# Two blocks on one core: whole Gram products and picked column sums in the delta heads, and an earlier load of gate rows in the first mixer

## Chip, cores and metric

The kernel runs on one core of a Trainium2 chip. The metric is device time in microseconds of one execution. TensorE (PE) multiplies, VectorE (DVE), ScalarE (ACT) and GpSimd (POOL) work element by element, SyncE (SP) issues most of the transfers. Every engine has its own instruction stream; they meet on semaphores.

## The reference

A sequence of 1024 tokens of width 1024 goes through two blocks in fp32, each a mixer and an MLP with residual. The first mixer is a forgetting attention (8 heads of width 64, with a cumulated gate added to the scores) beside a spatial gating unit. The second has a short convolution, a gated delta rule (4 heads of width 128, chunks of 64 tokens) and stick-breaking attention. What matters here, for one delta head and one chunk:

```python
k_beta = k * beta[..., None]
lower = where(strict, einsum('cd,sd->cs', k_beta, k) * decay, 0)
sol = triangular_solve(lower + eye, concat([v * beta, k_beta * exp(g)]))
u, w = sol[..., :Dv], sol[..., Dv:]
attn_intra = where(causal, einsum('cd,sd->cs', q, k) * decay, 0)
```

q and k are scaled to unit length first: l2norm(x) = x * rsqrt(sum(x*x) + eps). The kernel folds these scales and the decay into exponentials of sums of logarithms.

## The kernel before

The kernel is a row of stages. Projections and MLPs split fp32 weights into a high and a low part (GpSimd) and multiply in three products. Between them stand the first mixer (mix1_stage) and the delta stage (delta_stage).

**First mixer.** The attention is done in 32 units, four pairs of heads (hp 0 to 3) by eight query tiles. For a unit TensorE computes scores (L585), VectorE adds the gate rows and takes the row minimum (L723), ScalarE exponentiates, TensorE transposes, and every four units it multiplies with the values. The gate rows of a pair lie in cb[hp % 2], two buffers, and are loaded by SyncE (L564). The four slices of the next projection's weights (early_raw, L569) go to where q of the first pairs lay. SyncE's order is: rows of pair 0, rows of pair 1, a wait for unit 15's scores, the four slices, rows of pair 2, rows of pair 3; the rows of pair 2 have a wait of their own for unit 7, those of pair 3 for unit 15.

**Delta stage.** A head's 1024 tokens lie in 8 tiles of 128, each two chunks of 64. The inverse of each 64x64 triangular matrix is built in levels of doubling block size. X and XT hold the inverse and its transpose, LT the transposed matrix (rows 0 to 63 the even chunk, 64 to 127 the odd one), LQ the corner between the two chunks, and LM0/LM1 LT masked for one level. The inverse is carried on to 128 tokens (XT_whole), with level 6 for the corner. In level j TensorE makes t (X times LM, "t10" is level 1, first half), ScalarE copies it to T1, TensorE makes x and xt (L2246), VectorE subtracts them from X and XT (L2196, L2200; in level 5 into XT_whole, L2204, in level 6 L2208). Each level is done in two halves g = 0, 1 of four tiles.

The work of head h + 1 that prepares its matrices is put by hand into slots (j, g) of head h, in one table per engine (PE_SLOTS, ACT_SLOTS, DVE_SLOTS), with separate lists for head 0 (PE_FIRST and so on) and for a head's end (PE_END). GpSimd runs through POOL_EV. Since each engine works in its order, a waiting instruction holds up all that is behind it. The names used later:

- sqk, sqq: squares of k and q. ssk, ssq: their column sums spread to all rows, by a product with ones (L2235). ssc: the column sums of k squared, one column per tile (L2266). lns: their logarithm.
- g, gb: the gates spread to all rows (L2235, L2275, L2277); gcopy, gbcopy: their copies Gb, GBb. lnk, lnq: logarithms of ssk and ssq in Kb and Qb (L2049).
- rk, rq: -0.5 times the logarithm plus the gates (L2142, L2130). b: four pieces of 8 columns in small. elt0, elt: the exponentials of GBb (L2088).
- ea on VectorE: Qb plus the causal mask (L2152); ea0, ea on ScalarE: its exponentials. er1: exponential of Qb to Gb.
- kk: the Gram products of k (L2306). kq: of k with q (L2314). LT: kk times GBb (L2173). a_t: kq times Qb (L2158). qe: q times Gb.
- kt, vt: transposes of k and v; ktcopy: the copy to kd. vb: v times beta. xi: X from XT by transposing (L2296). w, u: the products with XT_whole (L2255). m1 to m5: the masked LM (L2025), ke, kd: scalings of kd, all on GpSimd.

Banks of PSUM: t in 0 and 1, x in 2 and 3, xt in 4 and 5, the preparation's results in 6 and 7, except kk in 2 and 3; xi is in bank 2. In head 0, ea of both engines stands in level 1 (ACT_LATE, DVE_LATE), and VectorE's next instruction there, a_t, needs it.

## Time and profile before

| | |
|---|---|
| median of 3 runs | 2767.29 us (2765.95 to 2768.79) |
| profiled execution, time | 2766.32 us |
| profiled execution, span from first to last instruction | 2764.6 us |
| mean granted TensorE clock | 0.980 of full |
| delta stage: head 0 to 1, 1 to 2, 2 to 3 (first block product to the next) | 57.32, 50.73, 47.87 us |

Busy time is the sum of an engine's instruction durations. In a timeline a row is a run of equal instructions: start in us from the span's start, time that they cover, engine, line, operation, output and inputs, count, and in brackets the idle time before and what ended it. A product of fp32 operands shows as two records. Times of single rows come from the one profiled execution.

### The profile page before, as it was taken

What the parts mean: (1) busy time and instruction counts of PE and PEld (TensorE: products, weight loads), DVE (VectorE), ACT (ScalarE), POOL (GpSimd) and SP (SyncE); (2) the same over time, 40 slices, a digit from 0 to 9 for tenths busy, and PEclk for the clock granted to TensorE, in tenths of its full rate; (3) what the DMA queues carried; (4) which work ended last, traced back from release to release, by engine and by line L of the source; (5) the groups of instructions that cost most, each with busy time, mean ns of one, the idle gap of its engine ahead of it and who ended that gap; (6) DMA issues with size and microseconds to landing.
All of it is one profiled execution on the core that took longest, in us unless ns stands there. A gap on an engine that the chain in (4) does not pass through costs nothing. (4 is left out here: it accounts for less than half of the span.)

```text
span 2764.6 us, 37035 instructions
## 1 busy us (share of the span) xinstructions
PE 2653.8 (96%) x14091; PEld 2113.2 (76%) x14091; DVE 1232.5 (45%) x1701; ACT 669.8 (24%) x1321; POOL 1143.1 (41%) x909
## 2 busy tenths in 40 slices
PE   7999789999999999999999979898999999999998
PEld 6786447888888888887888767853788888888877
DVE  3133343323333333353743044566125566666658
ACT  3201552200000000024231344465122111111123
POOL 4341135244444444543555322211324555555553
PEclk9999989999999999999999978999999999999999
DMA  3111103111111111121111000000311111111111
GB/s 132 43 50 38 47 1 122 31 46 46 47 51 46 49 49 49 53 89 61 46 46 50 12 2 2 17 1 1 122 31 54 46 49 49 49 49 47 48 57 76
DMA packets 91025, 131.75 MB, mean 48 GB/s; under 512 B 9269, under 2 KB 57632, under 8 KB 90920
## 3 DMA queue, kind: packets, MB, share of 16 engines
q1 hardware_dynamic: 88288, 121.76, 14.7%
q10 hardware_dynamic: 2632, 8.51, 0.8%
q8 instruction: 75, 1.23, 0.2%
q14 instruction: 30, 0.25, 0.0%
HBM read 121.82 MB, written 8.42 MB: 47 GB/s over the span
## 5 line engine op out<-in xcount | busy, mean ns | idle before, releaser
L115 POOL TENSOR_TENSOR w_hi<-w_raw,zero 128x512 fp32r<-128x512 f32 x320 | 380.1, 1188 | 994.5 <-PE bank L1095 450.5
L1093 PE MATMUL bank<-xt_hi,w_hi 128*128 128x512 f32 x1232 | 479.4, 389 | 0.8 <-DVE x_sb L1326 0.8
L1094 PE MATMUL bank<-xt_lo,w_hi 128*128 128x512 f32 x1232 | 479.3, 389 | 0.0
L1095 PE MATMUL bank<-xt_hi,w_lo 128*128 128x512 f32 x1232 | 479.3, 389 | 0.0
L117 POOL TENSOR_TENSOR w_lo<-w_raw,w_hi 128x512 fp32r<-128x512 f32 x320 | 464.9, 1453 | 25.1
L1430 DVE TENSOR_TENSOR x_sb<-bank,x_sb 128x512 f32<-128x512 f32 x320 | 221.2, 691 | 203.5 <-PE bank L1129 203.2
L1093 PEld LDWEIGHTS bank<-xt_hi,w_hi 128*128 128x128 f32 x1232 | 231.2, 188 | 49.2 <-DVE x_sb L1326 1.2
L1095 PEld LDWEIGHTS bank<-xt_hi,w_lo 128*128 128x128 f32 x1232 | 231.2, 188 | 48.0
L1094 PEld LDWEIGHTS bank<-xt_lo,w_hi 128*128 128x128 f32 x1232 | 231.2, 188 | 48.0
L1388 DVE COPY hidden_raw<-bank 128x512 f32<-128x512 f32 x44 | 30.4, 692 | 326.0 <-PE bank L1095 325.9
L178 PE MATMUL bank<-xt_hi,w_hi 128*128 128x512 f32 x448 | 174.6, 390 | 0.0
L178 PE MATMUL bank<-xt_hi,w_lo 128*128 128x512 f32 x448 | 174.3, 389 | 0.0
L178 PE MATMUL bank<-xt_lo,w_hi 128*128 128x512 f32 x448 | 174.3, 389 | 0.0
L1397 DVE SCALAR_TENSOR_TENSOR hidden_conv<-hidden_raw_conv,cols,hidden_conv 128x1024 f32<-128x1024 f32 x80 | 156.0, 1979 | 6.6 <-ACT hidden_conv L1230 1.3
L1127 PE MATMUL bank<-w_hi,hidden_hi 128*128 128x512 f32 x320 | 124.5, 389 | 0.0
L1128 PE MATMUL bank<-w_hi,hidden_lo 128*128 128x512 f32 x320 | 124.5, 389 | 0.0
L1127 PE MATMUL bank<-w_hi,hidden_hi_conv 128*128 128x512 f32 x320 | 124.5, 389 | 0.0
L1128 PE MATMUL bank<-w_hi,hidden_lo_conv 128*128 128x512 f32 x320 | 124.5, 389 | 0.0
L1129 PE MATMUL bank<-w_lo,hidden_hi 128*128 128x512 f32 x320 | 124.5, 389 | 0.0
L1129 PE MATMUL bank<-w_lo,hidden_hi_conv 128*128 128x512 f32 x320 | 124.5, 389 | 0.0
L1222 ACT ACTIVATE hidden_raw<-bank 128x512 f32<-128x512 f32 x44 | 26.3, 599 | 360.9 <-PE bank L1095 360.9
L1388 DVE COPY hidden_raw_conv<-bank 128x512 f32<-128x512 f32 x44 | 30.3, 691 | 165.7 <-PE bank L1095 165.7
(535 smaller groups left out, 4814.7 us busy)
## 6 DMA issues: line engine op xcount, KB each, us to landing
w_raw<-in_w_gate_up_dram SPq DMA_DIRECT2D x88, 256.0 KB, 3.1
w_raw<-in_w_ffn_up_dram SPq DMA_DIRECT2D x88, 256.0 KB, 3.1
w_raw<-in_w_mix_in_dram SPq DMA_DIRECT2D x56, 256.0 KB, 2.7
w_raw<-in_w_down_dram SPq DMA_DIRECT2D x44, 256.0 KB, 2.6
w_raw<-in_w_ffn_down_dram SPq DMA_DIRECT2D x44, 256.0 KB, 2.5
w_raw<-in_w_in_dram SPq DMA_DIRECT2D x40, 256.0 KB, 2.7
x_sb<-in_x_dram SPq DMA_DIRECT2D x4, 1024.0 KB, 8.3
gate_rows<-gate_sums SPq DMA_DIRECT2D x8, 512.0 KB, 6.8
```

The source lines that it names most:

```text
L115: pool.tensor_tensor(m.w_hi[:, u, :], m.w_raw[:, u, :], zeros, ALU.add).then_inc(m.hi_done, 1)
L117: pool.tensor_tensor(m.w_lo[:, u, :], m.w_raw[:, u, :], m.w_hi[:, u, :].bitcast(F32), ALU.subtract).then_inc(m.split, 1)
L178: mm = pe.matmul(m.psum[b][:, :], lhs, rhs, start=k == 0 and i == 0, stop=k == KD - 1 and i == 2)
L1093: pe.matmul(m.psum[b][:, :], u_hi[:, col], m.xt_hi[:, k, tok], start=k == 0, stop=False)
L1094: pe.matmul(m.psum[b][:, :], u_hi[:, col], m.xt_lo[:, k, tok], start=False, stop=False)
L1095: mm = pe.matmul(m.psum[b][:, :], u_lo[:, col], m.xt_hi[:, k, tok], start=False, stop=k == KD - 1)
L1127: pe.matmul(m.psum[bank][:, :], hi[:, j, tok], w_hi[:, u, :], start=j == 0, stop=False)
L1128: pe.matmul(m.psum[bank][:, :], lo[:, j, tok], w_hi[:, u, :], start=False, stop=False)
L1129: mm = pe.matmul(m.psum[bank][:, :], hi[:, j, tok], w_lo[:, u, :], start=False, stop=j == 1)
L1388: dve.tensor_copy(raw[:, 2 + j, PAD + h * HALF:PAD + (h + 1) * HALF], m.psum[2 * q_ + 1][:, :]).then_inc(ev_d, 1)
L1397: ins = dve.scalar_tensor_tensor(mix[:, c, :], raw[:, c, PAD - back:PAD - back + S], weights_of(i, c, 2 - back), mix[:, c, :], ALU.mult, A ...
L1430: dve.tensor_tensor(xs, m.psum[t][:, :], xs, ALU.add).then_inc(dn_ev, 1)
```

## The change

In the delta stage:

- kk becomes 8 products of 128x128 (both chunks of a tile and the corner at once, in banks 2 and 3, by tile) instead of 24 of 64 columns. LT and LQ then read their blocks out of them, each in two halves by bank. LQ is an event of its own, last in the start of a head; the x products of level 1, which write banks 2 and 3 again, wait for it.
- ssc and its logarithm on ScalarE go. Instead VectorE multiplies Kb (the logarithms, the same in all rows) by the identity and adds up each 128 columns, which picks the diagonal (lns).
- level 0's mask for XT moves to GpSimd (m0), ahead of m1; VectorE keeps the subtraction from the identity.
- ea writes to a buffer of its own (Qm) instead of Qb, and moves from slot (6,0) to (5,0). In head 0 it moves from level 1 to before xi.
- xi goes to bank 6, and kq waits for its copy.
- the slots close up: g, gb, ssk, ssq, kt, vt come half a level or more earlier on TensorE.

In the first mixer, SyncE issues the gate rows of pair 2 ahead of the four slices.

```diff
-            if hp == 1:
+            if hp == 2:
                 sp.wait_ge(scored, at_piece[(15, 1, 1)] + 1)
                 for u in range(RING):
                     sp.dma_start(early_raw[:, u, :], w_out(u)).then_inc(m.loaded[u], 16)
...
-    PE_SLOTS = {(2, 0): [("ssc", 1)], (2, 1): [("g", 1)], (3, 0): [("gb", 1)], (3, 1): [("ssk", 1)],
-                (4, 0): [("ssq", 1)], (4, 1): [("kt", 1)], (5, 0): [("vt", 1)], (6, 0): [("kk", 1)]}
-    ACT_SLOTS = {(1, 0): [("sqk", 1)], (1, 1): [("sqq", 1)], (2, 0): [("lns", 1)], (2, 1): [("gcopy", 1)],
-                 (3, 0): [("gbcopy", 1)], (3, 1): [("lnk", 1)], (4, 0): [("lnq", 1)], (4, 1): [("ktcopy", 1), ("elt0", 1)],
-                 (5, 0): [("elt", 1), ("ex", 1)], (5, 1): [("er1", 1)], (6, 1): [("ea0", 1), ("ea", 1)]}
-    DVE_SLOTS = {(1, 0): [("a_t", 0)], (1, 1): [("qe", 0)], (3, 0): [("gsum", 1)], (3, 1): [("b", 1)], (4, 0): [("rk", 1)],
-                 (4, 1): [("rq", 1)], (5, 0): [("vb", 1)], (5, 1): [("LT", 1)], (6, 0): [("ea", 1)]}
-    PE_FIRST = ["ssk", "ssc", "kk", "ssq", "kt", "vt", "xi", "kq"]
-    ACT_FIRST = ["lnk", "lns", "lnq", "ktcopy", "elt0", "elt", "ex", "er1", "xi"]
-    DVE_FIRST = ["gsum", "rk", "b", "LT", "XT", "rq", "vb"]
-    ACT_LATE, DVE_LATE = {(1, 0): ["ea0", "ea"]}, {(1, 0): ["ea"]}
+    PE_SLOTS = {(2, 0): [("g", 1)], (2, 1): [("gb", 1)], (3, 0): [("ssk", 1)], (3, 1): [("ssq", 1)],
+                (4, 0): [("kt", 1)], (4, 1): [("vt", 1)], (6, 0): [("kk", 1)]}
+    ACT_SLOTS = {(1, 0): [("sqk", 1)], (1, 1): [("sqq", 1)], (2, 0): [("gcopy", 1)], (2, 1): [("gbcopy", 1)],
+                 (3, 0): [("lnk", 1)], (3, 1): [("lnq", 1)], (4, 0): [("ktcopy", 1)], (4, 1): [("elt0", 1)],
+                 (5, 0): [("elt", 1)], (5, 1): [("ex", 1), ("er1", 1)], (6, 0): [("ea0", 1)], (6, 1): [("ea", 1)]}
+    DVE_SLOTS = {(1, 0): [("a_t", 0)], (1, 1): [("qe", 0)], (2, 1): [("gsum", 1)], (3, 0): [("lns", 1)], (3, 1): [("b", 1), ("rk", 1)],
+                 (4, 0): [("rq", 1)], (4, 1): [("vb", 1)], (5, 0): [("ea", 1)], (5, 1): [("LT", 1)]}
+    PE_FIRST = ["ssk", "kk", "ssq", "kt", "vt", "xi", "kq"]
+    ACT_FIRST = ["lnk", "lnq", "ktcopy", "elt0", "elt", "ex", "er1", "ea0", "ea", "xi"]
+    DVE_FIRST = ["gsum", "rk", "lns", "b", "rq", "LT", "XT", "LQ", "ea", "vb"]
...
-    DVE_END = [("XT", 1)]
+    DVE_END = [("XT", 1), ("LQ", 1)]
...
-    POOL_EV = [(h, n) for h in range(HG) for n in ("m1", "m2", "ke", "m3", "kd", "m4", "m5")]
+    POOL_EV = [(h, n) for h in range(HG) for n in ("m0", "m1", "m2", "ke", "m3", "kd", "m4", "m5")]
...
+                if h:
+                    pe_at(pool, h, "kk")
+                pool.tensor_tensor(XT[:, :, :], LT[:, :, :],
+                                   levels[:, 0, :].unsqueeze(1).to_broadcast([P, NT, B]), ALU.mult).then_inc(pool_s, 1)
...
+                elif n == "lns":
+                    act_at(dve, h, "lnk")
+                    if h:
+                        dve_at(dve, h - 1, "a_t")
+                    step(dve.tensor_tensor(Qm[:, :, :], Kb[:, :, :], m.ident[:, :].unsqueeze(1).to_broadcast([P, NT, P]), ALU.mult))
+                    dve.tensor_reduce(small[:, 1, :], Qm[:, :, :], AX, ALU.add).then_inc(dve_s, 1)
...
-                    act_at(dve, h, "er1")
-                    dve.tensor_tensor(Qb[:, :, :], Qb[:, :, :], mask[:, :].unsqueeze(1).to_broadcast([P, NT, P]),
+                    dve_at(dve, h, "rq")
+                    dve_at(dve, h, "lns")
+                    dve.tensor_tensor(Qm[:, :, :], Qb[:, :, :], mask[:, :].unsqueeze(1).to_broadcast([P, NT, P]),
                                       ALU.add).then_inc(dve_s, 1)
...
-                    for rows, cols in DIAGONAL:
-                        ins = dve.tensor_tensor(LT[rows, :, :], blocks(m.psum[2], rows), GBb[rows, :, cols], ALU.mult)
+                    for c in range(2):
+                        for rows, cols in DIAGONAL:
+                            ins = dve.tensor_tensor(LT[rows, 4 * c:4 * c + 4, :], tiles(m.psum[2 + c])[rows, :, cols],
+                                                    GBb[rows, 4 * c:4 * c + 4, cols], ALU.mult)
                     ins.then_inc(dve_s, 1)
+                elif n == "XT":
+                    pool_at(dve, h, "m0")
+                    dve.tensor_tensor(XT[:, :, :], eyes, XT[:, :, :], ALU.subtract).then_inc(dve_s, 1)
...
-                if n == "ssc":
-                    if h:
-                        act_at(pe, h, "sqk")
-                        dve_at(pe, h - 1, "a_t")
-                    for c in range(NT):
-                        mm = pe.matmul(m.psum[bank][:, c:c + 1], k_sq[:, c * P:(c + 1) * P], ones[:, 0:1], start=True, stop=True)
-                    mm.then_inc(pe_s, 1)
...
-                    for to, a0, b0 in ((UPPER, 0, 0), (LOWER, B, B), (UPPER, 0, B)):
-                        for c in range(NT):
-                            mm = pe.matmul(m.psum[bank + (a0 != b0)][to, c * B:(c + 1) * B], k_[:, h, c * P + a0:c * P + a0 + B],
-                                           k_[:, h, c * P + b0:c * P + b0 + B], start=True, stop=True)
-                    mm.then_inc(pe_s, 1)
+                    by_chunk(bank, lambda out, tok: pe.matmul(out, k_[:, h, tok], k_[:, h, tok], start=True, stop=True))
                 else:
-                    if h:
-                        dve_at(pe, h, "vb")
-                    else:
-                        act_at(pe, h, "lnq")
+                    act_at(pe, h, "xi")
...
                         if j == 1:
+                            dve_at(pe, h, "LQ")
```

## Rows read from the trace of the kernel before

**Rows 1.** The page's busy time of TensorE: us, share of the span, instructions.

```profile
PE 2653.8 (96%) x14091; PEld 2113.2 (76%) x14091; DVE 1232.5 (45%) x1701; ACT 669.8 (24%) x1321; POOL 1143.1 (41%) x909
```

**Rows 2.** Windows of two delta heads: length, busy us by engine, clock, DMA.

```profile
1654.58:1705.31 50.73, 44.91 (x672) 37.93 (x671) 22.39 (x43) 21.01 (x48) 11.40 (x7) 0.83 0.01 2
1705.31:1753.18 47.87, 40.81 (x671) 34.03 (x670) 22.39 (x43) 21.01 (x48) 11.94 (x7) 0.93 0.01 2
```

**Rows 3.** VectorE's timeline in the first mixer: start, duration, group, idle before.

```profile
341.28 0.69 DVE L723 CUSTOM_DVE_ANT_0 scores<-bank,gate_rows 128x512 f32<-128x512 f32 x1 [9.07 <-DMA gate_rows<-gate_sums]
```

**Rows 4.** SyncE's queue in the first mixer.

```profile
331.63 1.76 SPq L569 DMA_DIRECT2D early_raw<-in_w_out_dram  x4
333.44 2.07 SPq L564 DMA_DIRECT2D gate_rows<-gate_sums  x4
```

**Rows 5.** TensorE's timeline, first mixer: scores of units 8, 16, 17, 24.

```profile
293.85 1.99 PE L585 MATMUL bank<-k,q 64*128 64x512 f32 x8
...
331.59 1.99 PE L585 MATMUL bank<-k,q 64*128 64x512 f32 x8
...
342.64 3.36 PE L585 MATMUL bank<-k,q 64*128 64x512 f32 x8 [8.40 <-DVE min L723]
...
379.61 1.99 PE L585 MATMUL bank<-k,q 64*128 64x512 f32 x8
```

**Rows 6.** TensorE's timeline, delta: head 0, then level 3 of head 2.

```profile
1577.96 2.65 PE L2306 MATMUL bank<-qkv 128*64 128x64 f32 x48
...
1597.26 1.15 PE L2246 MATMUL bank<-X,LM 64*64 64x64 f32 x32
...
1607.29 1.12 PE L2246 MATMUL bank<-X,LM 64*64 64x64 f32 x16 [6.22 <-DVE XT L2200]
...
1616.47 1.54 PE L2246 MATMUL bank<-X,LM 64*64 64x64 f32 x32
...
1716.67 1.37 PE L2246 MATMUL bank<-X,LM 64*64 64x64 f32 x32
```

**Rows 7.** TensorE's timeline, delta, head 2 and the turn to head 3.

```profile
1710.70 1.95 PE L2266 MATMUL bank<-ones,k_sq 128*128 128x1 f32 x16
...
1723.09 1.37 PE L2246 MATMUL bank<-X,LM 64*64 64x64 f32 x32
...
1741.24 1.14 PE L2246 MATMUL bank<-XT_whole,T 64*64 64x64 f32 x16
...
1748.34 1.15 PE L2296 MATMUL bank<-eye_block,XT 64*64 64x64 f32 x32 [1.63 <-DVE LT_corner L2182]
...
1751.30 1.95 PE L2314 MATMUL bank<-qkv 128*128 128x128 f32 x16
```

**Rows 8.** VectorE's and ScalarE's timelines at the start of the delta stage.

```profile
1577.74 1.23 DVE L2142 SCALAR_TENSOR_TENSOR GBb<-Kb,GBb 128x1024 f32<-128x1024 f32 x1 [1.57 <-ACT Kb L2049]
...
1589.46 1.63 DVE L2181 TENSOR_TENSOR XT<-eye_block,XT 128x512 f32<-128x512 f32 x1
...
1600.04 2.67 DVE L2152 TENSOR_TENSOR Qb<-Qb,mask 128x1024 f32<-128x1024 f32 x1
...
1602.74 2.44 ACT L2088 ACTIVATE Qb<-Qb,small 128x128 f32<-128x128 f32 x8 [3.90 <-DVE Qb L2152]
```

**Rows 9.** VectorE's timeline, delta, head 2.

```profile
1722.84 0.42 DVE L2196 TENSOR_TENSOR X<-X,bank 128x256 f32<-128x256 f32 x1 [2.19 <-PE bank L2246]
...
1733.27 0.85 DVE L2204 TENSOR_TENSOR XT_whole<-XT,bank 64x256 f32<-64x256 f32 x2
...
1746.87 0.69 DVE L2181 TENSOR_TENSOR XT<-eye_block,XT 128x512 f32<-128x512 f32 x1
```

**Rows 10.** ScalarE's and GpSimd's timelines, delta, heads 2 and 3.

```profile
1715.27 1.09 ACT L2049 ACTIVATE Gb<-bank 128x512 f32<-128x512 f32 x2 [2.32 <-PE bank L2235]
...
1722.22 1.27 ACT L2049 ACTIVATE Kb<-bank,eps 128x512 f32<-128x512 f32 x2 [2.07 <-PE bank L2235]
...
1754.42 1.27 POOL L2025 TENSOR_TENSOR LM<-LT,levels_block 128x512 f32<-128x512 f32 x1 [5.11 <-PE bank L2246]
```

More of the change, by code:

```diff
@@ L1870, with program_order @@
 SBD = 64
-def program_order(first, late, slots, level, ends):
+def program_order(first, slots, level, ends):
     events = [(0, n) for n in first]
@@ L1880, in program_order @@
             events += level(h, *key)
-            events += [(0, n) for n in late.get(key, ()) if h == 0]
             events += [(h + ahead, n) for n, ahead in slots.get(key, ()) if h + ahead < HG]
@@ L1898, in delta_stage @@
     X, XT, LT, LQ, T1 = (at(n, [P, NT, B], 64 + 2 * i) for i, n in enumerate(("X", "XT", "LT", "LT_corner", "T1")))
[L1899 removed]
+    whole, ke, Qm = (at(n, [P, NT, P], 76 + 4 * i) for i, n in enumerate(("XT_whole", "ke", "q_decay")))
     q_sq, k_sq, gc, gcb, gct, gbt, beta = (gates[n] for n in ("q_sq", "k_sq", "gc", "ab", "gct", "gbt", "beta"))
@@ L1928, in delta_stage @@
-    BANK = {"ssk": 4, "ssc": 6, "kk": 2, "ssq": 6, "kt": 0, "vt": 4, "kq": 6, "xi": 2}
+    PE_SLOTS = {(2, 0): [("g", 1)], (2, 1): [("gb", 1)], (3, 0): [("ssk", 1)], (3, 1): [("ssq", 1)],
[3 more added lines that the diff above has]
+                 (5, 0): [("elt", 1)], (5, 1): [("ex", 1), ("er1", 1)], (6, 0): [("ea0", 1)], (6, 1): [("ea", 1)]}
@@ L2227, in _ @@
                     start(h + 1, "XT")
+                    start(h + 1, "LQ")
         @block.tensor
```

48 lines of the change are left out of this document (19 added, 29 removed).

## Prediction

> **What bounds the kernel now.** The page comes first. TensorE is busy 96% of the span [rows 1], so a change counts where it lets TensorE do less, wait less, or run at the higher of its two clock levels (2.4 against 1.2 GHz, a granted clock of 1.0 against 0.5). The change touches two places, the first mixer near 330 us and the delta stage from about 1573 to 1780 us, and there TensorE is not 96% busy in the sense of working steadily. The windows of two whole delta heads, cut where one head's first block product starts and where the next one's does, give 50.73 and 47.87 us with TensorE busy 44.91 and 40.81 us, at a granted clock of 0.83 and 0.93 [rows 2]. The two windows run one and the same list of instructions, so 2.9 us between them is the clock alone. The waits that count are read in the timeline of TensorE.
>
> In the mixer VectorE sits 9.07 us before it may take up score unit 16, the first of the third pair, and what ends the wait is the load of its gate rows [rows 3]. SyncE's queue shows why: the four slices of the projection are issued at 331.63 and the gate rows only behind them, at 333.44 [rows 4]. Both stand behind the wait for unit 15, although the buffer of the third pair's rows is free after unit 7. TensorE then idles 8.40 us on VectorE [rows 5].
>
> In the delta stage I read three places: the start of head 0, where TensorE idles 6.22 us before the second half of level 2 [rows 6]; the middle of a head, with its single-column products; and the turn from head to head, where the next head's first transpose (xi) starts 7.10 us after the Gram products (kk) are done [rows 7].
>
> **The gate rows.** The four requests for early_raw and the two for the third pair's rows change places. Issued when TensorE is at unit 8, at about 295 us [rows 5], instead of 333 us, the rows land long before they are wanted: the nearest bound is 341.28 - 333.44 = 7.8 us from issue to use [rows 3, 4], with the slices in front and the fourth pair's rows in the same queue, against 37 us up to 332.2, when VectorE would take them. Nothing stands in the queue between them that could be delayed. The slices go out on the same wait for unit 15 as before. The fourth pair's rows still stand behind them; that pair begins at 379.61 on TensorE [rows 5], 46 us after its rows were issued, and this slack stays. What the wait is worth is shown by the mixer itself. From unit 8 to unit 16 TensorE goes 331.59 - 293.85 = 37.74 us, from unit 16 to unit 24 it goes 379.61 - 331.59 = 48.02 us [rows 5], with equal work. The difference of 10.3 us is more than the 8.40 of idle, since the products behind the gap take 3.36 us where the same ones take 1.99, at the lower clock. I take 10.3; the bounds are 8.4 (idle only) and 11.
>
> **Delta heads, middle.** Out goes the single-column product (ssc), 16 records of TensorE in 1.9 us [rows 7] per head. In comes, on VectorE, a product of Kb with the identity and a sum over each 128 columns. The first has a row in kind: two SBUF operands of 128x1024 take 1.23 us [rows 8]. No add-reduction of this size stands in the trace; below it is bounded by half of that, above by the 2.67 us of the slowest 128x1024 operation here; I take 1.2, as one pass over as many elements. The pair, 2.5 us with the hand-over between the two, lies in slot (3,0). VectorE idles 2.19 us there before the next update [rows 9], and TensorE's wait on the banks (below) adds 0.5 to that cover. So the pair costs nothing, but with hardly 0.1 us to spare; at the upper bound it costs 1.3 us per head.
>
> The Trainium skill speaks against this piece: "VectorE: DVE Perf Modes", in its decision table, says to expect tensor_reduce at 1x and calls it the slowest VectorE operation, to be restructured when hot. No row here shows one. One element a cycle is what the 1.23 us of [rows 8] already are, so by the rule the sum stands unchanged unless the cover fails.
>
> The slots closed up, and with them come waits that were not there. A pair of banks is read by ScalarE in 1.09 us (gate rows) or 1.27 us (logarithm) [rows 10], and the next use of those banks now comes half a level later instead of a whole one. Half a level of products is 0.98 us (in [rows 7] and [rows 10]: the logarithm starts at 1722.22, the level's products are over at 1723.09, after which ssq would have to wait until 1723.5). With about 0.1 for each hand-over this gives stalls of 0.45 (gb behind g), 0.5 (ssq behind ssk) and 0.3 (vt behind kt); an old stall of 0.3 before kt goes away. Net 0.95 us to pay.
>
> **Delta heads, turn.** The Gram products go from 24 of 64 columns (2.65 us for 48 records, [rows 6]) to 8 of 128, the form of kq (1.95 us, [rows 7]): 0.7 us. At the lower clock the gain is less, at most it is 0.9. Behind them, with K the end of kk: LT in four pieces instead of two, 2 x 0.85 = 1.7 us by the row of a 64x256 PSUM operation [rows 9], to K + 1.8. Then the two updates of XT_whole, 0.42 each, with the mask addition (ea) no longer between them. On GpSimd m0 takes 1.27 us [rows 10], to K + 3.15. Then VectorE's subtraction: 0.69 us alone [rows 9], 1.63 us where GpSimd works on LM beside it [rows 8]. GpSimd goes straight on to m1, so I take 1.6: K + 4.8. xi starts at K + 4.85 instead of K + 7.10. Gain 2.25 us; bounds 3.0 (TensorE's own work, with the two decayed products up to K + 4.3, becomes the bound) and 1.2. LQ comes after and is hidden by xi, u and kq. kq now waits for the copy of xi out of bank 6 (0.6 us, half of the copied pair of [rows 10]), hidden by u, which has kq's form and count and so its 1.95 us [rows 7]. ea moves to slot (5,0), in place of v times beta; it takes 1.23 us there if it has no GpSimd work beside it [rows 8], and what it replaces is two PSUM operations of 128x512, each between 0.42 and 0.84 by [rows 9], so that I book nothing (bounds 0.4 either way). The exponentials behind it have all of level 6. Without that cover they would hold up w by their 2.44 us [rows 8].
>
> The rule behind those 1.6 us is in the Trainium skill, "SBUF — State Buffer", on the shared port pair: a VectorE operation with two SBUF inputs and a GpSimd operation exclude each other for a whole instruction. By it the subtraction waits out m1, 1.27 + 0.69 = 1.96 us, and xi starts at K + 5.2. The 1.63 beside 0.69 agrees with the rule in kind.
>
> Per head: 1.88 + 0.7 + 2.25 - 0.95 = 3.9 us, three times (heads 1 to 3 are prepared, the last one prepares none): 11.6.
>
> **Delta start.** Before, ea and its exponentials stood inside level 1 of head 0, and a_t waited for them. Now they stand before xi. From t10 to the first product of level 3 head 0 takes 1616.47 - 1597.26 = 19.2 us, head 2 takes 1716.67 - 1705.31 = 11.4 us for the same [rows 2, 6]: 7.8 us come back (6.22 of it is the idle time, the rest lower clock). Against it stands a later t10. VectorE is through rk at 1578.97 [rows 8], with the pair at 1581.4, with the four small pieces of b at 1582.3 (0.9 assumed, at most 4 x 0.42). GBb's exponentials take 2.44 [rows 8]: 1584.8. LT 1586.5, m0 1587.9, subtraction 1589.6, LQ 1590.4. ea beside GpSimd takes up to 2.67 [rows 8]: 1592.9. Its exponentials, 2.44: 1595.3. Copy of xi: 1595.9. kq, at half clock after that much idle time, 3.5: t10 at 1599.4 instead of 1597.26 [rows 6], 2.1 late. Another 0.6 for level 1 at half clock. Gain 5.1, bounds 2 (ea and the pair at their dearest, slow clock for 5 us more) and 8 (ea uncontended, kq at full clock).
>
> **Sum.** 10.3 + 5.1 + 11.6 = 27.0 us off. The profiled execution took 2766.3 us (span 2764.6), so 2739.3; the runs' median lies 1.0 above it: 2740.3 us.
>
> **Rivals.**
> (a) The forecast, within some 7 us.
> (b) The clock goes with it. The heads were at 0.83 and 0.93 [rows 2]; with less waiting they run at 1.0, which the difference of the two windows prices at 2.9 us for 0.10, so 5 + 2 us in the two heads and some in head 0: 10 us more, 2730. For it: the long idle stretches go. Against it: the stalls before the XT_whole pieces stay, and new ones of 0.3 to 0.5 come.
> (c) VectorE becomes the bound: the pair at 3.9 us instead of 2.5 (reduction at its upper bound) delays each head by 1.3 and the start by 1.4, and the turn comes out at its lower bound of 1.2: 1.3 x 3 + 1.4 + 1.05 x 3 = 8.5 us back, 2749.
> (d) The rows are hidden anyway, or the mixer finds another wait: the probabilities' copies on ScalarE bind instead, and only about half comes, 5 us back: 2745. Against: units 8 to 16 ran at that pace without the wait.
> (e) Slower: the three new bank stalls in levels 2 to 4 drop the clock there for most of every head. Levels 2 to 5 are some 24 us at full clock (1710.70 to 1741.24 less kk and the stalls, [rows 7]) and cost up to 24 more at half, 72 for three heads, which ends at 2812. It decides from 27 us of added time, that is 9 us a head or 18 us at half clock. Against: in [rows 2] whole heads with stalls up to 1.6 us still average 0.83 or more. The Trainium skill, "TensorE: Matmul & The Clock Gate", Part 1, says that idle TensorE is what lowers the clock; here the products after the 8.40 us gap ran at the lower level [rows 5], while a gap of 1.63 us was followed by xi at full speed [rows 7].
> (f) The change does nothing measurable: both effects cancelled, within 0.2% (5.5 us), which is about what a measurement of this kernel can tell from no change. It would need 22 us of new waits.
>
> **Numbers.** Chances: (a) 0.52, (b) 0.17, (c) 0.14, (d) 0.10, (f) 0.03, (e) 0.04. The time is that of (a), 2740.3. The range runs from (b) with the turn at its better bound, 2728, to (c) with the start at its worse bound, 2752. Faster by over 0.2%: 0.93; within: 0.03; slower: 0.04.
>
> **What would show it.** In the mixer: no wait of VectorE on gate_rows over 1 us, unit 16 to unit 24 in about 37.7 us on TensorE. In the delta stage: kk with 16 records of 128x128; the identity product and the reduction on VectorE in slot (3,0), 1.2 us each, and no TensorE wait on the update of XT in the second half of level 3; xi about 4.9 us after kk; stalls of 0.3 to 0.5 before gb, ssq and vt; no wait over 1.5 us in head 0 between t10 and level 3; heads of about 47 and 44 us. The prediction is wrong if the reduction takes over 2 us, if a head's granted clock falls below 0.75, or if t10 of head 0 comes after 1602 less the mixer's 10.

## The result, and the profile after

The changed kernel takes 2723.86 us (median of four runs, 2719.99 to 2726.05), against 2766.62 for the kernel before (2765.05 to 2768.79): a ratio of 0.9843, 95% interval [0.9826, 0.986], or 42.8 us less. The forecast was 2740.3 us with a range of 2728 to 2752. The direction was right, the gain was 16 us larger than forecast, and the time lies outside the range, below its lower end.

The profiled execution took 2724.72 us, its span is 2722.9. The page's busy times, against [rows 1]:

```profile
PE 2625.4 (96%) x13899; PEld 2089.7 (77%) x13899; DVE 1237.4 (45%) x1717; ACT 669.2 (25%) x1317; POOL 1147.4 (42%) x913
```

TensorE has 192 instructions fewer and is busy 28.4 us less. VectorE's share of the span did not move. The 42 us are to be looked for by stretch. I cut the delta stage at the first ssk product (its start), at the first block product t10 of each head, and at the scan's first product. The windows of the changed kernel: start, heads 0, 1 and 2, and head 3 up to the scan. Columns as in [rows 2].

```profile
1563.48:1587.83 24.35, 12.92 (x88) 10.31 (x88) 12.85 (x20) 10.98 (x26) 16.46 (x27) 0.75 0.01 1
1587.83:1631.27 43.44, 38.65 (x624) 32.59 (x623) 24.02 (x47) 21.10 (x47) 12.05 (x8) 0.90 0.01 2
1631.27:1672.69 41.42, 36.52 (x623) 30.38 (x622) 24.02 (x47) 21.10 (x47) 12.10 (x8) 0.96 0.01 2
1672.69:1714.16 41.47, 36.59 (x624) 30.37 (x623) 24.01 (x47) 21.10 (x47) 12.06 (x8) 0.96 0.01 2
1714.16:1743.64 29.48, 25.87 (x545) 23.55 (x544) 15.27 (x33) 7.71 (x17) 6.67 (x8) 0.94 0.01 2
```

Two windows of the kernel before, cut at the same products, which [rows 2] do not have: head 0, and head 3 up to the scan.

```profile
1597.26:1654.58 57.32, 46.07 (x672) 39.22 (x671) 25.06 (x44) 23.34 (x56) 11.02 (x7) 0.79 0.01 2
1753.18:1781.09 27.91, 24.29 (x545) 22.02 (x545) 15.28 (x33) 7.70 (x17) 6.67 (x8) 1.00 0.01 2
```

Laid beside each other (us; "forecast" is what the prediction's terms give for the stretch):

| stretch | before | after | difference | forecast |
|---|---|---|---|---|
| program start to first ssk product | 1574.36 | 1563.48 | -10.9 | -10.3 |
| ssk to t10 of head 0 | 22.90 | 24.35 | +1.5 | +2.1 |
| head 0 | 57.32 | 43.44 | -13.9 | -11.1 |
| head 1 | 50.73 | 41.42 | -9.3 | -3.9 |
| head 2 | 47.87 | 41.47 | -6.4 | -3.9 |
| head 3 up to the scan | 27.91 | 29.48 | +1.6 | 0 |
| scan to the end | 983.51 | 979.26 | -4.3 | 0 |
| sum (span) | 2764.6 | 2722.9 | -41.7 | -27.0 |

The last two rows run the same list of TensorE's instructions before and after. In head 3 the granted clock went from 1.00 to 0.94; in heads 0 to 2 it went from 0.79, 0.83 and 0.93 to 0.90, 0.96 and 0.96.

In the mixer no wait on gate_rows is left. TensorE's timeline, scores of units 8, 16 and 24, against [rows 5]:

```profile
294.03 1.99 PE L585 MATMUL bank<-k,q 64*128 64x512 f32 x8
...
330.96 1.99 PE L585 MATMUL bank<-k,q 64*128 64x512 f32 x8
...
368.70 1.99 PE L585 MATMUL bank<-k,q 64*128 64x512 f32 x8
```

From unit 16 to 24 it is 37.74 us, to the hundredth what the prediction read off units 8 to 16 of the kernel before. That it fits to the hundredth is luck: the same stretch takes 35.17 us in rows_only, which has the same mixer. The scores of unit 17 are no longer at half clock (1.78 us, before 3.36).

At the delta stage's start, against [rows 6], TensorE's timeline shows where its waits went:

```profile
1578.96 1.98 PE L2294 MATMUL bank<-eye_block,XT 64*64 64x64 f32 x32 [8.24 <-DVE XT L2182]
1584.12 3.78 PE L2305 MATMUL bank<-qkv 128*128 128x128 f32 x16 [3.19 <-ACT X L2081]
1587.83 1.90 PE L2251 MATMUL bank<-X,LM 64*64 64x64 f32 x32
...
1593.05 0.68 PE L2251 MATMUL bank<-X,LM 64*64 64x64 f32 x16 [0.98 <-DVE XT L2207]
...
1597.47 1.37 PE L2251 MATMUL bank<-X,LM 64*64 64x64 f32 x32
```

The 6.22 us in the middle of level 2 have become 0.98, the wait that each head has there. Level 3 begins 9.64 us after t10, where head 0 took 19.2 us before. VectorE's timeline of the same stretch, against [rows 8], has the pair (L2131, L2132), LT in four pieces, the subtraction and ea (the buffer Qm shows as q_decay):

```profile
1568.01 1.26 DVE L2131 TENSOR_TENSOR q_decay<-Kb,ident 128x1024 f32<-128x1024 f32 x1
1569.30 1.22 DVE L2132 TENSOR_REDUCE small<-q_decay 128x8 f32<-128x1024 f32 x1
...
1574.00 1.73 DVE L2177 TENSOR_TENSOR LT<-bank,GBb 64x256 f32<-64x256 f32 x4 [1.47 <-ACT GBb L2087]
1577.17 1.73 DVE L2182 TENSOR_TENSOR XT<-eye_block,XT 128x512 f32<-128x512 f32 x1 [1.45 <-POOL XT L2020]
...
1579.61 1.50 DVE L2155 TENSOR_TENSOR q_decay<-Qb,mask 128x1024 f32<-128x1024 f32 x1
```

Last, the turn between heads 2 and 3 on TensorE, against [rows 7]:

```profile
1701.32 3.04 PE L2302 MATMUL bank<-qkv 128*128 128x128 f32 x16
1704.30 1.71 PE L2251 MATMUL bank<-XT_whole,T 64*64 64x64 f32 x16
1706.73 2.02 PE L2260 MATMUL bank<-XT_whole,ke 128*128 128x128 f32 x16 [0.72 <-DVE XT_whole L2215]
1709.31 1.15 PE L2294 MATMUL bank<-eye_block,XT 64*64 64x64 f32 x32 [0.56 <-DVE XT L2182]
```

The group behind the Gram products (kk, L2302) starts at 1704.30, xi at 1709.31: 5.01 us, read in the same way as the 7.10 before; the forecast was 4.85. At the other two turns it is 5.42 and 5.83 us, with w's products (L2260) in between partly at the lower clock. And kk, which takes 2.05 us at the turn between heads 1 and 2, takes 3.04 here. That is the clock, and it is the subject of most experiments.

### The profile page after: what moved, and what is told of

Same layout as the page of the kernel before. It is cut to its first block and busy times, and to the rows that moved or that the text cites. A ratio compares the mean times of both kernels' runs of the same rounds, so it can differ in the third digit from the quotient of the medians.

```text
span 2722.9 us, 36671 instructions
## 1 busy us (share of the span) xinstructions
PE 2625.4 (96%) x13899; PEld 2089.7 (77%) x13899; DVE 1237.4 (45%) x1717; ACT 669.2 (25%) x1317; POOL 1147.4 (42%) x913
```

## The experiments

Four theories are named in the expectations. **W**: work and waits set the time of a stretch, at a clock that stays as it is for such work. **P**: the moment decides; which stretch falls to the lower clock level depends on where the waits lie in time, so that the same instructions can cost several us more or less. **S**: the thin products (single columns) are what brings the clock down behind them. **T**, against S: any further work at that place does it. Each run has one profiled execution, so every length of a head is a single reading. All times in us; "floor" is a whole head at a granted clock of 1.00: about 40.5 after the change (40.48 measured below), about 44.8 before it (an estimate: 47.87 for head 2, less 3.1 by which its groups at half clock are longer than the same groups elsewhere).

**1. The mixer's edit alone** (rows_only).

```
 (before)
-            if hp == 1:
+            if hp == 2:
                 sp.wait_ge(scored, at_piece[(15, 1, 1)] + 1)
```

> The kernel before with the gate rows' move alone. Theory W (each stage's clock follows from its own work and waits): the mixer loses 10.3 us and every later stage is as before, 2756.3 us, head lengths 57.3, 50.7 and 47.9 us. Theory P (TensorE's lower clock level falls on a stage also by when the stage comes, so that a shift alone moves time in unchanged stages): the mixer still loses 10.3 us, but the delta heads or the stage behind them change by 2 us or more with identical instructions, and the total ends more than 2 us from 2756.3.

Measured: 2754.78 (10 runs, 2744.70 to 2757.76), ratio 0.9963 [0.9947, 0.998], about 10 us less. Heads 57.30, 50.72, 47.87, the start 22.87, head 3 27.90, the rest 983.54: the delta stage is the kernel before to within 0.03 us. The delta stage begins 13.0 us earlier in this profile. The mixer's term stands, and here a shift of the whole delta stage in time leaves every low-clock stretch in it where it was.

**2. The delta stage's edits alone** (delta_only): the changed kernel with that one line as before.

```
 (after)
-            if hp == 2:
+            if hp == 1:
                 sp.wait_ge(scored, at_piece[(15, 1, 1)] + 1)
```

> The changed kernel with the gate rows behind the four slices again. By W the total is 2723.9 + 10.3 = 2734.2 us and the heads are 43.4, 41.4 and 41.5 us as in the changed kernel. By P the heads or the stage behind them differ from those by 2 us or more, and the total lies more than 2 us from 2734.2. The recorded prediction would have had 2750.6.

Measured: 2735.69 (2735.24 to 2738.59), ratio 0.991 [0.9881, 0.9938]. Heads 43.43, 41.92, 43.02 at 0.90, 0.92, 0.92; start 24.36; the rest 981.99. By the two ratios the parts are worth 10 and 25 us alone and 43 together, but the interval of the 25 runs from 17 to 33, so that the 8 us between are not shown; by the medians this run is 11.8 us slower than the changed kernel, close to the mixer's 10.3. The delta stage has the same instructions in both, and yet head 1 is 0.5 us and head 2 1.6 us longer here, head 3 1.6 us shorter (27.91), and scan to end 2.7 us longer. So a shift of the whole stage can come with other single lengths too.

**3. The moment alone** (before_shift). Two more ssk products ahead of the delta stage of the kernel before, 1.9 us of TensorE's time, into a bank that is written again.

```
 (before)
             for n in PE_FIRST:
+                if n == "ssk":
+                    for c in range(2):
+                        pe.matmul(m.psum[BANK["ssk"] + c][:, :], ones[:, :], k_sq[:, c * HALF:(c + 1) * HALF], start=True, stop=True)
                 prepare(0, n)
```

> The kernel before with one more pair of column-sum products ahead of the first one in the delta stage (four records of 128x512, 1.9 us; it writes the same values to the same banks). By W 2766.6 + 1.9 = 2768.5 us, and the heads stay at 57.3, 50.7 and 47.9 us. By P the total ends more than 2 us away from 2768.5, and the granted clock of the heads moves.

Measured: 2762.95 (2759.9 to 2764.67), ratio 1.0002 [0.9989, 1.0015]. In the profile head 0 takes 58.46 (57.32), head 1 49.05 (50.73), head 2 the same, and scan to end 977.45 where the kernel before has 983.51 with the same instructions. The time of a stretch is not set by its own instructions alone. But the total does not refute W: the kernel before, measured beside it, has a median of 2763.77 (2755.82 to 2768.33), and the 1.9 us that W adds lie inside the interval of the ratio.

Whether the moment does it, or one execution simply differs from the next, can be seen ahead of the delta stage, where neither an edit nor an earlier stage differs. From the program's start to the first ssk product the twelve kernels with the earlier gate rows run the same code; their profiles take from 1559.70 to 1566.64 us there. The two windows:

```profile
0.00:1559.70 1559.70, 1517.16 (x7106) 1208.95 (x7106) 585.35 (x835) 330.69 (x621) 653.17 (x540) 1.00 0.18 53
0.00:1566.64 1566.64, 1524.48 (x7106) 1213.26 (x7106) 584.58 (x835) 331.10 (x621) 651.61 (x540) 0.99 0.18 53
```

(after_shift and dense_filler.) So 6 to 7 us between two profiles can arise in identical code from its first instruction on. The 6 us of scan to end may be no more than that, and no run here separates the two.

**4. The single-column products put back** (ssc_back), their result unused; and **5. the same time in dense products** (dense_filler), 8 of 128x128 in their place.

```
 (after, at the head of "g"; 5 has ones[:, :] and 128 columns for each c)
                     dve_at(pe, h - 1, "a_t")
+                    act_at(pe, h, "sqk")
+                    for c in range(NT):
+                        pe.matmul(m.psum[bank][:, c:c + 1], k_sq[:, c * P:(c + 1) * P], ones[:, 0:1], start=True, stop=True)
```

> The changed kernel with the single-column products put back on TensorE in heads 1 to 3, in front of the gates in slot (2,0); their result is not read. At full clock they cost 3 x 1.9 = 5.6 us: 2729.5 us. Theory S (these products, which fill the array little, are what lowered the clock in levels 1 and 2 of heads 1 and 2 before, where about 1.5 to 2 us a head were lost): the spells of 0.5 in level 2 come back and the total is 2733 to 2737 us. Without S level 2 runs at full clock.

> The changed kernel with products of the same count, the same weights (squares of k) and the same place as the single-column ones of ssc_back, but 128 columns wide; nobody reads them. At full clock they cost a little more than 1.9 us each time (kq's form, 1.95 us): 5.8 us, 2729.7 us. Theory S (single-column products lower the clock because they hardly move data through the array): level 2 keeps its full clock here, heads about 45.4, 43.4 and 43.4 us. The other theory T (any further work at this place lengthens the stretch or moves it so that the clock falls): the spells at 0.5 in level 2 stand here too and the heads are as in ssc_back, 46.6, 46.7 and 46.1 us.

Measured: 2735.54 (2733.93 to 2739.38), ratio 0.9907 [0.9878, 0.9937], and 2735.91 (2733.18 to 2738.23), ratio 0.9894 [0.9877, 0.991]. By the medians both are 12 us slower than the changed kernel, for 3 x 1.88 = 5.6 us of work. The heads are 46.56, 46.68, 46.07 with the thin ones (0.87, 0.89, 0.89) and 43.74, 46.65, 44.91 with the dense ones (0.94, 0.85, 0.92). In the thin variant the clock falls right at them in head 1; TensorE's timeline:

```profile
1637.07 0.68 PE L2251 MATMUL bank<-X,LM 64*64 64x64 f32 x16 [0.97 <-DVE XT L2207]
1637.69 2.83 PE L2270 MATMUL bank<-ones,k_sq 128*128 128x1 f32 x16
1640.37 1.01 PE L2240 MATMUL bank<-gate_thirds,sel 96*128 96x512 bf16 x2
1641.32 1.12 PE L2251 MATMUL bank<-T,XT 64*64 64x64 f32 x16
```

(0.61 and 0.68 are what the last two take at full clock.) That looks like S, and the same stretch in the other variant decides it. The windows run from the second half of level 2 to level 3, first in head 1 of ssc_back_shift (run 6), then in head 1 of dense_filler_shift (run 7):

```profile
1638.31:1645.82 7.51, 7.51 (x102) 5.52 (x104) 2.34 (x5) 2.51 (x5) 1.64 (x1) 0.77 0.01 2
1642.06:1648.35 6.29, 6.13 (x103) 4.82 (x104) 2.34 (x5) 2.35 (x5) 1.64 (x1) 1.00 0.01 3
```

Same place, same count, same weights, same wait of 0.97 us before. With the thin products the stretch takes 7.49 to 9.09 us at 0.62 to 0.77 in all six heads of the two runs; with the dense ones it takes 6.29 or 6.30 us at 1.00 in all six. At this place S is borne out and T is not: the thin products cost at least 1.2 us a head in clock. Yet the medians of 4 and 5 are alike. The three heads together take 139.3 with the thin ones and 135.3 with the dense ones; what the dense ones save there is hidden by 5.3 us more ahead of the stage, in identical code, and 2.0 more in scan to end. And 135.3 is still above the 132.2 that the expectation had by S, because the clock falls elsewhere, at the turns between heads.

**6. and 7. Both again, 1.9 us later** (ssc_back_shift, dense_filler_shift), and **8. the changed kernel 1.9 us later** (after_shift), with the edit of 3.

> ssc_back with the same 1.9 us ahead, a second sample at another moment: theory S expects about 139 us again for the three heads (46.6, 46.7, 46.1 before), with a low clock in level 2 of each, 2737.5 us; if the moment decides, 135 to 143.

> dense_filler with the same 1.9 us ahead. Theory S expects less for the heads than with single-column products: below 134 us for the three, as one head without a low stretch in level 2 already had (43.7 us) and the two others had one by chance. Theory T expects 135 to 139 us, level 2 at 0.5 in two or three heads.

> The changed kernel with the extra 1.9 us of column-sum products ahead of the delta stage's first ones. Where a stretch of the lower clock is set by the work around it alone: 2725.8 us, heads 43.4, 41.4 and 41.5 us, and 979.3 us from the scan's first product to the end. Theory P: one of these lengths changes by over 1 us, and the sum with it.

Measured: 2740.09 (2736.94 to 2741.29), ratio 0.9908 [0.9893, 0.9923]; 2735.32 (2734.09 to 2737.94), ratio 0.9888 [0.9873, 0.9903]; 2723.53 (2721.3 to 2725.55), ratio 0.9847 [0.9834, 0.9861]. For after_shift the start is 26.62 instead of 24.35, and head 0 takes 41.40 instead of 43.44: what was added in front was given back behind. ssc_back_shift has heads of 45.54, 45.09 and 46.08, together 136.7 where S expected about 139; dense_filler_shift has 44.88, 45.27 and 43.28, together 133.4, below the 134 that S gave as its bound and below T's 135 to 139. These two ran side by side, and the thin one is 4.8 us slower in the median. The medians of a kernel stay within 5 us of its shifted version, while single heads move by up to 2 us. The moment may decide at which turn the clock falls; with one profile each, this is not told apart from the scatter of executions.

**9. All but one of the single-column products taken out of heads 1 to 3 of the kernel before** (before_thin_ssc).

```
 (before; lns becomes a copy for heads 1 to 3)
-                    for c in range(NT):
+                    for c in range(1 if h else NT):
```

> The kernel before with seven of the eight single-column products of heads 1 to 3 left out (the logarithms of head 0 stand in for the missing sums, so those heads are scaled wrongly). At full clock this takes 14 of 16 records, 1.65 us a head, 4.9 us in all, off: 2761.7 us if it starts from 2766.6. If these products also cost clock in the kernel before, level 2 of heads 1 to 3 runs at 1.0 and 8 to 14 us go. If the gain of the change comes from less waiting elsewhere, hardly more than 4.9 us.

Measured: 2758.68 (2754.24 to 2759.58), ratio 0.9969 [0.9958, 0.998]: 7.6 us less, for 3 x (1.95 - 0.38) = 4.7 us of work. Heads 55.70, 47.76, 47.78, scan to end 977.55. The heads give 4.7 (1.6, 3.0 and 0.1), head 3 takes 1.6 back, and the unchanged stage from scan to end gives 6.0; 1.9 are lost ahead of the delta stage, where nothing is changed either. Level 2's second half in heads 1 and 2 goes from 6.57 and 6.59 us at 0.74 to 3.52 at 1.00, of which 1.57 is work and 1.5 clock, as S expects. In head 2 as good as all of it is lost again: the clock falls at the end of that head, where it had not fallen before. The total, 7.6 us by the medians and 8.6 by the ratio, is at the lower end of the 8 to 14 that were expected by S.

**10. ea left out of head 0's middle, in the kernel before** (before_early_ea): the one stall that the prediction's start term was about, and no other edit of the change.

```
 (before)
-    ACT_FIRST = ["lnk", "lns", "lnq", "ktcopy", "elt0", "elt", "ex", "er1", "xi"]
-    DVE_FIRST = ["gsum", "rk", "b", "LT", "XT", "rq", "vb"]
-    ACT_LATE, DVE_LATE = {(1, 0): ["ea0", "ea"]}, {(1, 0): ["ea"]}
+    ACT_FIRST = ["lnk", "lns", "lnq", "ktcopy", "elt0", "elt", "ex", "er1", "xi", "ea0", "ea"]
+    DVE_FIRST = ["gsum", "rk", "b", "LT", "XT", "rq", "vb", "ea"]
+    ACT_LATE, DVE_LATE = {}, {}
```

> The kernel before with head 0's mask addition and its exponentials taken out of level 1 and put behind v times beta and behind xi's copy. The prediction priced this wait with its clock at 7.8 us, less what the earlier place costs. Here t10 of head 0 need not move, so: head 0 57.3 - 6.8 = 50.5 us, total 2766.3 - 6.8 = 2759.5 us. If the low clock stays after the short gaps at the stage's start: 5.3 us of pure wait go, 2761.

Measured: 2749.2 (2747.59 to 2751.9), ratio 0.9939 [0.9926, 0.9953] against 2767.01: 17.8 us less. The windows of heads 0, 1 and 2 and of head 3:

```profile
1598.44:1645.34 46.90, 39.32 (x671) 33.00 (x670) 22.38 (x43) 22.16 (x53) 11.94 (x7) 0.96 0.01 2
1645.34:1693.23 47.89, 40.84 (x672) 34.06 (x671) 22.38 (x43) 21.03 (x48) 11.94 (x7) 0.93 0.01 2
1693.23:1741.07 47.84, 40.79 (x672) 34.01 (x671) 22.38 (x43) 21.02 (x48) 11.95 (x7) 0.93 0.01 2
1741.07:1768.97 27.90, 24.29 (x546) 22.02 (x545) 15.25 (x33) 7.71 (x17) 6.68 (x8) 1.00 0.01 2
```

Its start took 22.89 us (22.90): nothing was paid in front. Head 0 gives back 10.4 us, of which 5.25 is idle time (6.22 to 0.97); its clock goes from 0.79 to 0.96. Head 1, with the same instructions as before and no edit in it, gives 2.8 (0.83 to 0.93), and scan to end takes 977.43 instead of 983.51. TensorE's timeline of head 0 shows the place of the old wait, and the thin products (L2266), behind which nothing falls here:

```profile
1603.74 0.68 PE L2246 MATMUL bank<-X,LM 64*64 64x64 f32 x16 [0.97 <-DVE XT L2200]
1604.35 1.95 PE L2266 MATMUL bank<-ones,k_sq 128*128 128x1 f32 x16
...
1608.82 1.37 PE L2246 MATMUL bank<-X,LM 64*64 64x64 f32 x32
```

From the second half of level 2 to level 3 this is 5.08 us at 1.00. In heads 1 and 2 of the same run the clock does fall behind the same products; their windows, and that of head 2 of the kernel before:

```profile
1650.12:1656.71 6.59, 6.59 (x98) 5.55 (x100) 2.35 (x5) 1.74 (x4) 1.64 (x1) 0.74 0.00 0
1698.00:1704.59 6.59, 6.59 (x98) 5.55 (x100) 2.35 (x5) 1.72 (x4) 1.64 (x1) 0.74 0.01 2
1710.08:1716.67 6.59, 6.59 (x98) 5.55 (x100) 2.50 (x5) 1.74 (x4) 1.64 (x1) 0.74 0.01 4
```

So in the kernel before and its variants the thin products of a head came with 1.5 us of lost clock, as a rule and not always.

**11. The pair's cost doubled** (lns_twice): the reduction done twice.

```
 (after)
+                    step(dve.tensor_reduce(small[:, 1, :], Qm[:, :, :], AX, ALU.add))
                     dve.tensor_reduce(small[:, 1, :], Qm[:, :, :], AX, ALU.add).then_inc(dve_s, 1)
```

> The changed kernel with the reduction done twice, 1.2 us more of VectorE in slot (3,0) and at the start. The prediction said that the pair fits the cover with hardly 0.1 us to spare. If so, each prepared head gets 1.1 to 1.3 us longer and the start 1.2: 2728.5 us, with a wait of TensorE on the update of XT after the second half of level 3. If there is more cover than that, heads keep 43.4, 41.4 and 41.5 us and only the start grows.

Measured: 2732.24 (2730.67 to 2735.79), ratio 0.9882 [0.9865, 0.9898], 8.4 us slower than the changed kernel. The start is 1.8 us longer (26.17). In each of heads 0 to 2 a new wait of TensorE stands in level 4, here in head 0:

```profile
1609.48 0.63 PE L2252 MATMUL bank<-X,LM 64*64 64x64 f32 x16
1611.12 0.68 PE L2252 MATMUL bank<-X,LM 64*64 64x64 f32 x16 [1.01 <-DVE XT L2208]
```

So the cover was used up by the pair, as the prediction said: once costs nothing, and of the second 1.22 us nearly all (1.01) shows. That makes 3 x 1.0 + 1.8 = 4.8, the forecast. The profiled execution (2735.79, the slowest of the four) is 11.2 us longer than the changed kernel's; besides the 4.8 it has 3.1 more ahead of the stage and 3.9 more in scan to end (983.20), both in unchanged code, and 1.6 less in head 3.

**12. and 13. Where ea stands** (ea_first: before LT at the start; ea_back: back in its old slot within a head).

```
 (after; ea_first, then ea_back)
-    DVE_FIRST = ["gsum", "rk", "lns", "b", "rq", "LT", "XT", "LQ", "ea", "vb"]
+    DVE_FIRST = ["gsum", "rk", "lns", "b", "rq", "ea", "LT", "XT", "LQ", "vb"]
...
-                 (4, 0): [("rq", 1)], (4, 1): [("vb", 1)], (5, 0): [("ea", 1)], (5, 1): [("LT", 1)]}
+                 (4, 0): [("rq", 1)], (4, 1): [("vb", 1)], (5, 1): [("LT", 1)], (6, 0): [("ea", 1)]}
```

> The changed kernel with head 0's mask addition on VectorE moved ahead of LT, where VectorE idles 1.47 us. ScalarE can then exponentiate before xi is copied, and the 3.19 us that TensorE idles before kq should go down to the copy, about 0.7: 2.5 us less, 2721.4 us, t10 of head 0 at 21.8 us after the first product of the stage instead of 24.35. If the clock stays low longer instead (the stretch before is idle either way), 1 us less or nothing.

> The changed kernel with the mask addition of heads 1 to 3 back in slot (6,0), between the two updates of XT_whole; the buffer of its own stays. Forecast from the prediction's steps: the wait before the last product of level 6 falls from 1.8 to about 0.6 us, but the second update waits 1.2 to 1.9 us behind the addition, the subtraction and the copies of w and xi with it, so xi comes 6.1 us after kk instead of 5.0: 0 to 1.2 us a head, 2724 to 2728 us. If the new slot was worth nothing: 2720 to 2724.

Measured: 2726.2 (2722.66 to 2727.78), ratio 0.9864 [0.9847, 0.988], and 2721.84 (2719.1 to 2722.76), ratio 0.9844 [0.9828, 0.9861]. ea_first shortens the start as foreseen (21.86, 2.5 less), and the heads take it back: 45.13, 40.48, 43.34 at 0.84, 1.00, 0.88. Its head 1 is the measured floor of 40.5. In ea_back the waits only change their place, as the corner of XT_whole is now earlier and the late piece and xi later; TensorE's timeline at the turn from head 0 to head 1:

```profile
1620.42 1.13 PE L2260 MATMUL bank<-XT_whole,ke 128*128 128x128 f32 x8 [1.29 <-DVE XT_whole L2215]
1622.63 1.16 PE L2260 MATMUL bank<-XT_whole,ke 128*128 128x128 f32 x8 [1.08 <-DVE XT_whole L2215]
1623.98 1.15 PE L2294 MATMUL bank<-eye_block,XT 64*64 64x64 f32 x32 [0.19 <-DVE XT L2182]
```

The new slot of ea is worth nothing that can be measured.

**14. The old Gram products** (old_kk): 24 of 64 columns (48 records), LT in two pieces, the rest as changed.

```
 (after)
-                    by_chunk(bank, lambda out, tok: pe.matmul(out, k_[:, h, tok], k_[:, h, tok], start=True, stop=True))
+                    for to, a0, b0 in ((UPPER, 0, 0), (LOWER, B, B), (UPPER, 0, B)):
+                        for c in range(NT):
+                            mm = pe.matmul(m.psum[bank + (a0 != b0)][to, c * B:(c + 1) * B], k_[:, h, c * P + a0:c * P + a0 + B],
+                                           k_[:, h, c * P + b0:c * P + b0 + B], start=True, stop=True)
+                    mm.then_inc(pe_s, 1)
```

> The changed kernel with the Gram products in their old form, 24 of 64 columns, and LT and LQ reading them as before. By the prediction's steps 0.7 us more for TensorE at head 0 and in each prepared head, 0.3 us less for LT: 2723.9 + 0.4 to 0.7 x 4 = 2725.5 to 2726.7 us. If the narrow products also lower the clock (they stand in the stretch behind a 1.8 us wait where it fell most often): 2 us a head, 2730 or more.

Measured: 2721.24 (2718.0 to 2724.08), ratio 0.9835 [0.9822, 0.9848]. Heads 42.67, 40.73, 40.74, the last two at 1.00. The kk products take 2.65 us instead of 2.05, but LT is two pieces and no longer four, and the wait before w's product shrinks from 1.29 to 0.95 us:

```profile
1659.70 2.65 PE L2300 MATMUL bank<-qkv 128*64 128x64 f32 x48
1662.28 1.14 PE L2247 MATMUL bank<-XT_whole,T 64*64 64x64 f32 x16
1664.38 2.02 PE L2256 MATMUL bank<-XT_whole,ke 128*128 128x128 f32 x16 [0.95 <-DVE XT_whole L2211]
```

A head at full clock is 40.73 with the old form and 40.48 with the new one. The whole Gram products are worth 0.25 us a head, which does not show in the time.

**15. The parts that helped, together** (best): ea_first, ea_back, and GpSimd's first LM product behind VectorE's subtraction.

```
 (after, beside the edits of 12 and 13)
                 for j in LEV[:-1]:
+                    if j == 1:
+                        dve_at(pool, h, "XT")
```

> The changed kernel with three edits: head 0's mask addition ahead of LT (2.5 us off the start by the run ea_first), the mask additions of the other heads back in slot (6,0) (a shorter wait before level 6's last product, by the run ea_back), and GpSimd starting m1 only when VectorE's subtraction is done, so that this takes 0.7 instead of 1.7 us (1.0 off the start, up to 0.6 a head). By the waits 2723.9 - 2.5 - 1.0 - 3 x 0.3 = 2719.5 us. If the clock takes back what the waits give, as it seems to have done in ea_first, 2722 to 2726.

Measured: 2719.75 (2714.84 to 2720.53), ratio 0.9831 [0.9817, 0.9844]; start 20.82, heads 40.38, 42.44, 39.94 at 0.98, 0.92, 1.00, in a profiled execution that is the fastest of the five. It is the fastest in the median of all, by 4 us against the changed kernel, with intervals of the ratio that overlap. VectorE's and GpSimd's timelines show what the last edit does:

```profile
1574.39 0.69 DVE L2184 TENSOR_TENSOR XT<-eye_block,XT 128x512 f32<-128x512 f32 x1 [1.45 <-POOL XT L2020]
...
1575.16 2.49 POOL L2029 TENSOR_TENSOR LM<-LT,levels_block 128x512 f32<-128x512 f32 x2 [0.80 <-DVE XT L2184]
```

The subtraction takes 0.69 instead of 1.73 us. The Trainium skill, "SBUF — State Buffer", on the shared port pair, says that a VectorE operation with two SBUF inputs and a GpSimd operation exclude each other for the whole instruction. The pair of numbers agrees in kind: 1.73 is 1.04 longer, most of the 1.27 of the GpSimd operation beside it.

## Why the prediction was off in size

**The mixer: right.** 10.3 forecast; about 10 by the ratio of the edit alone, and 10.3 from unit 16 to 24 in this pair of profiles. The same stretch gives 12.9 between the kernel before and rows_only, and 8.1 between delta_only and the changed kernel. The price of the wait was 8.4 idle and 2 of clock, and the neighbouring pair of units, which ran without it, was the right yardstick, to some 2.5 us.

**The turn: right in work.** 5.01 us from kk to xi against 4.85 at the turn with the least clock lost between them, 5.42 and 5.83 at the others. The subtraction took 1.73 beside GpSimd (1.6 taken).

**The pair: right.** 1.22 + 1.22 us, and no wait of TensorE on it; doubled, it costs. The upper bound of 2.67 for the reduction, on which rival (c) rested, was far off. The rule weighed against the piece (the Trainium skill, "VectorE: DVE Perf Modes", decision table) expects tensor_reduce at 1x and calls it the slowest VectorE operation. The reduction was no slower here than a product of the same size, so that the measurement does not bear out the second half.

**The bank stalls: too dear.** 0.45, 0.5 and 0.3 forecast before gb, ssq and vt; measured 0.16, 0.28 and none, so that the net 0.95 us a head became 0.16. The old one before kt is gone as foreseen. Against that, kk's 0.7 us were worth 0.25 (old_kk). At full clock the forecast gives a head of 44.8 - 3.9 = 40.9, and 40.48 was measured: the work term of a head was right to 0.4 us, by errors that nearly cancel.

**The failed step is the clock, held as it was in two terms.** The first and larger is "Delta start": "7.8 us come back (6.22 of it is the idle time, the rest lower clock)". It priced the wait by the stretch from t10 to level 3 and held the clock of everything behind it as before. The wait alone, taken out of the kernel before, is worth 17.8 us by the medians (before_early_ea; 13 to 20 by the interval of the ratio), where the forecast for it was 6.8: 10.4 in head 0, 2.8 in head 1, which has no edit, and 6.1 in scan to end, with 1.2 lost ahead of the stage. The 13.2 in the two heads are twice the forecast; the 6.1 are no larger than what identical code shows ahead of the stage.

The second is the first term of "Delta heads, middle": the single-column products were booked as "16 records of TensorE in 1.9 us", with nothing for the clock behind them. In heads 1 and 2 before, level 2's second half took 6.57 and 6.59 us at 0.74 where 5.08 is its time at 1.00 (head 0 of before_early_ea). That is 1.5 us a head on top of the work. It is gone in the changed kernel, where that stretch runs at 1.00 in all three heads (4.42, 4.42 and 4.41 us).

In heads 0 to 2 together, 29.6 us came off. By the floors of 44.8 (an estimate) and 40.5 these are 5.3 of idle time, 13.0 of work and 11.4 of clock. The prediction had 6.2, 11.7 and 1.0. So its work was right to 1.3 us and its idle time to 1.0, and the clock is the miss. Of the 14.7 us that the profile gained beyond the forecast, 10.7 lie in these heads, 4.3 in scan to end, 1.2 in mixer and start, less 1.6 lost in head 3. The 4.3 in scan to end belong to no edit.

**The rivals.** (b), the clock goes with it, was the right mechanism, with a chance of 0.17 and a price of 10 us; in the three heads the clock gave 11.4, of which the forecast had 1.0. Its argument against itself, that stalls stay, does not hold: the changed kernel still has two stalls in each head, 1.79 us in level 6 and 0.72 to 1.29 before w, and runs at 0.90 to 0.96. (e), the clock falls through new small stalls, did not come: 0.16 and 0.28 us of them, at 0.96. (c), (d) and (f) fell with the rows above.

**What stays open.** At which turn between heads the clock falls, and why there. W in its strict form is refuted, since the same instructions took 43.44 and 41.40 us (head 0 of the changed kernel and of after_shift), and head 1 of before_early_ea has no edit. P is neither shown nor refuted. The kernel before and rows_only agree in every head to 0.03 us although the stage is 13 us earlier, while delta_only and the changed kernel, also the same stage at another moment, differ by 1.6 us in heads 2 and 3. With one profile for each kernel this cannot be told from differences between executions, and a second and third profile of the same kernel would have been the experiment. S is borne out in level 2: the clock fell behind a whole set of thin products in 14 of 15 heads with the short wait of 0.97 us before them, and in none of the 32 heads with dense products, a single thin one or none in their place. It is not shown that a kernel's total moves by as much, since the clock saved in level 2 was in part lost again at a turn. Edits whose forecast was right in work (ea_first 2.5 us, ssc_back 5.6 us) came out at -2 and at +12 us in the time, so a term of under some 5 us in this stage can be neither promised nor refuted by the time of the whole kernel.

## What to carry to other kernels

A wait of several us on TensorE in the middle of dense work costs more than its length: here 6.2 us of it cost 10.4 in its own head and 2.8 in the next one. Where a change removes one, price it by the whole head against a head without it (57.3 against 47.9 gave 9.4), and let the range reach down by half as much again. Ask of every group of products that goes not only how long it took, but what clock the groups behind it had: the thin products took 1.9 us and came with another 1.5. When two variants tie in total time, compare the granted clock at the place of the edit before calling a theory dead. And look at unchanged stretches first when comparing two profiles: what moves there is the size below which no part of the rest can be assigned.

## What the runs showed of the hardware

- The stretch from the scan to the end, with the same instructions in all these kernels, took from 977.4 us (before_early_ea, before_shift) over 979.3 (the changed kernel) to 983.5 (the kernel before, rows_only). Nothing in it was changed. The stretch ahead of the delta stage, also unchanged, took from 1559.7 to 1566.6 us in the twelve kernels with the earlier gate rows, and from 1570.7 to 1576.2 in the five without.
- An add-reduction of 128x1024 to 128x8 takes VectorE 1.22 us, the same as the product of that size beside it.
- A product with a single column costs TensorE as much as one of 128: 16 records of 128x1 in 1.95 us, 16 of 128x128 in 1.95 us [rows 7]. What follows it differs: in the six heads with these thin products in level 2 of the changed kernel the granted clock of that stretch was 0.62 to 0.77, in the six with dense ones 1.00.
- VectorE's subtraction of 128x512 takes 0.69 us alone and 1.73 us beside a GpSimd product.
